# Two transformer blocks on one core: later-key sums of the first attention as three-row products in the short format, and the attention bias negated by ScalarE

## The reference

```python
for o in range(n):                      # key blocks of 128, nearest first
    z = einsum('bhnqd,bhnkd->bhnqk', qb[:, :, o:], kb[:, :, :n - o])
    log_rest = log_sigmoid(-z)
    if o == 0: log_rest = where(diag_mask, log_rest, 0.0)
    after = einsum('bhnqj,js->bhnqs', log_rest, after_mat) + carry[:, :, o:, :, None]
    w = exp(log_sigmoid(z) + after)
    ...
    carry = carry.at[:, :, o:].add(sum(log_rest, axis=-1))

scores = where(valid, scores + bias, -inf)     # chunked attention
```

## Time and profile before

| | |
|---|---|
| median of 3 runs | 697.48 us (697.42 to 697.54) |
| profiled execution, its own time | 697.37 us |
| its span | 695.6 us |
| mean granted TensorE clock | 0.998 |
| TensorE busy (PE) | 687.7 us, 99% |
| VectorE, ScalarE, GpSimd busy | 481.5, 406.3, 94.3 us |
| chain that ended last | PE 94%, POOL 2%, ACT 2%, DVE 1% |

### The profile page before, as it was taken

One profiled execution on the slowest core, in us unless ns is written; L12 is line 12 of the kernel. 1 busy time (PEld: TensorE's weight loads), 2 busy tenths in 40 slices (PEclk: granted clock), 3 DMA queues, 4 the chain that ended last, 5 costly groups with the idle time before them and its releaser, 6 DMA issues.

```text
span 695.6 us, 9577 instructions
## 1 busy us (share of the span) xinstructions
PE 687.7 (99%) x3890; PEld 594.3 (85%) x3890; DVE 481.5 (69%) x717; ACT 406.3 (58%) x680; POOL 94.3 (14%) x150
## 2 busy tenths in 40 slices
PE   9999999999999999999999999999999999999996
PEld 8888888888888888888888888998888888888885
DVE  6887687767666666667365767766668877777774
ACT  7776664657445555546555857554467665556553
POOL 2143022588200000002320000000000000000001
PEclk9999999999999999999999999999999999999999
DMA  9935533746555555536434334555454555445401
GB/s 342 387 122 207 217 119 125 256 175 216 203 186 184 188 197 203 196 122 221 175 126 175 122 122 182 189 183 201 155 188 175 191 214 200 182 182 183 180 1 60
DMA packets 19483, 126.13 MB, mean 181 GB/s; under 512 B 2416, under 2 KB 2544, under 8 KB 5232
## 3 DMA queue, kind: packets, MB, share of 16 engines
q1 hardware_dynamic: 19296, 125.34, 49.2%
q10 hardware_dynamic: 144, 0.20, 0.1%
HBM read 124.48 MB, written 1.05 MB: 180 GB/s over the span
## 4 chain that ended last, share of the span: by engine, by line
PE 94%; POOL 2%; ACT 2%; DVE 1%; issue 0%; POOLq 0%
PE bank L222 91%; PE bank L231 3%; POOL rtmp L243 1%; POOL qtok L243 0%; POOL ktok L243 0%; ACT whi L234 0%; DVE sc L1251 0%; DVE yy L251 0%; DVE xres L243 0%; DVE yy L243 0%; ACT L234 0%; ACT xa L234 0%; DVE wlo L243 0%; ACT sc L234 0%; ACT uT L234 0%
## 5 line engine op out<-in xcount | busy, mean ns | idle before, releaser
L243 DVE TENSOR_TENSOR wlo<-raw,whi 128x1024 fp32r<-128x1024 f32 x222 | 271.8, 1236 | 62.1 <-ACT whi L234 59.4
L234 ACT ACTIVATE whi<-raw 128x1024 fp32r<-128x1024 f32 x222 | 230.2, 1051 | 2.5 <-PE bank L222 2.1
L222 PE MATMUL bank<-xb,whi 128*128 128x512 f32 x496 | 124.3, 393 | 0.3 <-DVE sg L243 0.2
L222 PE MATMUL bank<-xa,whi 128*128 128x512 f32 (+1 forms) x496 | 115.7, 365 | 0.0
L222 PEld LDWEIGHTS bank<-xb,whi 128*128 128x128 f32 x496 | 90.4, 188 | 18.1 <-DVE sg L243 0.4
L222 PEld LDWEIGHTS bank<-xa,whi 128*128 128x128 f32 x496 | 87.4, 189 | 13.7
L222 PE MATMUL bank<-whi,xb 128*128 128x512 f32 (+1 forms) x352 | 96.5, 355 | 0.0
L222 PEld LDWEIGHTS bank<-xb,wlo 128*128 128x128 f32 x496 | 67.7, 190 | 4.9
L222 PEld LDWEIGHTS bank<-whi,xb 128*128 128x128 f32 x352 | 62.1, 189 | 9.3 <-ACT vtok L234 0.3
L222 PE MATMUL bank<-xa,wlo 128*128 128x256 f32 x432 | 69.4, 282 | 0.0
L222 PE MATMUL bank<-xb,wlo 128*128 128x256 f32 x496 | 69.1, 282 | 0.0
(11 more groups left out here) (235 smaller groups left out, 898.5 us busy)
## 6 DMA issues: line engine op xcount, KB each, us to landing
raw<-in_w_dram SPq DMA_DIRECT2D x109, 1024.0 KB, 4.8
first<-in_first_dram SPq DMA_DIRECT2D x8, 388.0 KB, 6.1
raw<-in_w_dram SPq DMA_DIRECT2D x4, 512.0 KB, 8.1
bias<-in_bias_dram SPq DMA_DIRECT2D x1, 1024.0 KB, 8.5
xres<-in_x_dram SPq DMA_DIRECT2D x1, 1024.0 KB, 6.8
gain<-in_ffn_norm_w_dram SPq DMA_DIRECT2D x1, 512.0 KB, 8.3
gain<-in_mix_norm_g_dram SPq DMA_DIRECT2D x1, 512.0 KB, 9.1
gain<-in_ffn_norm_g_dram SPq DMA_DIRECT2D x1, 512.0 KB, 5.3
```

What stands on the lines that cost most here:

```text
L222: return P(lambda e: e.matmul(o, l, r, start=start, stop=stop), *w, inc=inc)
L234: return A(lambda e: e.activation(o, i, f, **kw), *w)
L243: return q(lambda e: e.tensor_tensor(out=o, in0=a, in1=b, op=op), *w)
```

## The change

For the sums over later keys, `tri` and `negs` are rounded once, at the start, to the short format (`tri_r`, `negs_r`, two GpSimd casts of 128x128). A new function `sb_parts(b)`, handed to `later` behind `sb_scores(b)`, makes a high part of each `L` on ScalarE (`L_h`) and a low part on VectorE (`L_l`), 128x384 each. `sb_after` then does four short products per head: `tri_r` and `negs_r` by the high part, `tri_r` and `negs_r` by the low part, the `tri_r` ones on 384 columns at once. `L_h` lies over zm and `L_l` over sp, and the first `tri` and `negs` lie where `wk0` is.

The bias is no longer negated by GpSimd before group 2, but by one ScalarE copy with scale -1 behind the last unit of group 3; the memset of its corner is queued there too.

```diff
-    tri = N("tri", [128, 128])
-    negs = N("negs", [128, 128])
+    tri_r = N("tri_r", [128, 128], F32R)
+    negs_r = N("negs_r", [128, 128], F32R)
...
+    wk_at = (N.lo + 511) // 512 * 512
+    tri, negs = [at(wk_at + 512 * i, n, [128, 128]) for i, n in enumerate(("tri", "negs"))]
     wk = [N(f"wk{i}", [128, 384]) for i in range(8)]
+    L_h, L_l = [[at(wk_at + (4 * i + j) * 1536, f"L{j}{i}", [128, 384], F32R) for i in range(2)] for j in range(2)]
...
+    def sb_parts(b):
+
+        for i in range(2):
+            h, L = 2 * b + i, wk[4 * i + 2]
+            sb["Lh", h] = copy(L_h[i][:, :], L[:, :], sb["L", h], sb["g", h])
+        for i in range(2):
+            h, L = 2 * b + i, wk[4 * i + 2]
+            sb["Ll", h] = low(L_l[i][:, :], L[:, :], L_h[i][:, :], sb["Lh", h])
...
-            mm(o[:, 0:256], tri[:, :], L[:, 0:256], True, False, sb["L", h], tri_tok, neg_tok, *bank_free[bank])
-            mm(o[:, 128:256], negs[:, :], L[:, 256:384], False, True)
-            p = mm(o[:, 256:384], tri[:, :], L[:, 256:384], True, True, inc=True)
+        for i in range(2):
+            h, gm, bank = 2 * b + i, wk[4 * i + 3], 4 + i
+            o, hi, lo = pb[bank], L_h[i], L_l[i]
+            mm(o[:, 0:384], tri_r[:, :], hi[:, :], True, False, sb["Lh", h], tri_tok, neg_tok, *bank_free[bank])
+            mm(o[:, 128:256], negs_r[:, :], hi[:, 256:384], False, False)
+            mm(o[:, 0:384], tri_r[:, :], lo[:, :], False, False, sb["Ll", h])
+            p = mm(o[:, 128:256], negs_r[:, :], lo[:, 256:384], False, True, inc=True)
...
-    g = ts(G, flat(bias[:, :, :]), flat(bias[:, :, :]), -1.0, None, ALU.mult, None, bias_ld)
-    bias_tok = memset(bias[0:64, :, 192:256], BIG, g)
     for n, _ in enumerate(group_1(2, qb)):
...
             sb_scores(0)
+            later(lambda: sb_parts(0))
...
             sb_scores(1)
+            later(lambda: sb_parts(1))
         elif n == 2:
             qn = q_scaled()
+        else:
+            a = copy(flat(bias[:, :, :]), flat(bias[:, :, :]), bias_ld, scale=-1.0)
+            bias_tok = memset(bias[0:64, :, 192:256], BIG, a)
```

More of the change, by code:

```diff
@@ L556, in two_block_program @@
     g = memset(tri[:, :], -1.0)
-    tri_tok = select(tri[:, :], [[-1, 128]], ALU.is_gt, 0.0, 0, 1, g)
-    neg_tok = memset(negs[:, :], -1.0)
+    g = select(tri[:, :], [[-1, 128]], ALU.is_gt, 0.0, 0, 1, g)
+    tri_tok = G(lambda e: e.tensor_copy(tri_r[:, :], tri[:, :]), g)
+    g = memset(negs[:, :], -1.0)
+    neg_tok = G(lambda e: e.tensor_copy(negs_r[:, :], negs[:, :]), g)
     g = memset(sbmask[:, :, :], 0.0)
@@ L647, in sb_scores @@
             zm, sp, L, gm = wk[4 * i:4 * i + 4]
-            sb["L", 2 * b + i] = stt(L[:, :], zm[:, :], 0.0, sp[:, :], ALU.max, ALU.add, sb["sp", 2 * b + i])
+            v = stt(L[:, :], zm[:, :], 0.0, sp[:, :], ALU.max, ALU.add, sb["sp", 2 * b + i])
             sb["g", 2 * b + i] = stt(gm[:, :], zm[:, :], 0.0, sp[:, :], ALU.min, ALU.subtract)
-    def sb_after(b):
[L653 to L656, removed]
-            mm(o[:, 0:256], tri[:, :], L[:, 0:256], True, False, sb["L", h], tri_tok, neg_tok, *bank_free[bank])
-            mm(o[:, 128:256], negs[:, :], L[:, 256:384], False, True)
-            p = mm(o[:, 256:384], tri[:, :], L[:, 256:384], True, True, inc=True)
+            sb["L", 2 * b + i] = v
+    def sb_parts(b):
[5 more added lines that the diff above has]
+            sb["Ll", h] = low(L_l[i][:, :], L[:, :], L_h[i][:, :], sb["Lh", h])
+    def sb_after(b):
+        for i in range(2):
[5 more added lines that the diff above has]
+            p = mm(o[:, 128:256], negs_r[:, :], lo[:, 256:384], False, True, inc=True)
             v = tt(V, gm[:, :], o[:, 0:384], gm[:, :], ALU.add, p, sb["g", h])
```

## The result

The changed kernel takes 699.42 us (median of 8 executions, 699.02 to 699.77) against 697.45 for the kernel before on the same chip (8 executions, 697.04 to 697.77): a ratio of 1.0028, 95% interval 1.0019 to 1.0038. It is 2.0 us slower. 697.9 was forecast, and the range ended at 698.7.

A forecast was written before the change was run, and what follows sets the result against it. TensorE's queue was taken as the bound up to 60 us. It saves 1.22 us but waits 1.65 at `sb_out(2)`, which starts 0.4 later: 697.37 + 0.4 = 697.8, or 697.9 against the median; range 696.2 to 698.7.

The forecast's parts named there:

- What bounds the kernel: Up to 60 us TensorE's queue is the clock; shorter products save their full length unless TensorE has to wait.
- Part 1, the products: TensorE's later-key blocks shrink from 1.75 to 1.14 us, saving 0.53 in the first and 0.61 in the second.
- the 1.22 of the sum: TensorE's whole saving: 1.14 us from both blocks plus 0.08 of waiting at the first `sb_out`.
- Part 2, the first pair: New ScalarE copies and VectorE subtractions before the first `sb_out` cost nothing; the cover holds by 0.7 us.
- Part 3, the second pair: The bias copy in ScalarE's queue delays the Exps; TensorE waits 1.65 us at `sb_out(2)`, starting 0.4 us later than before.
- Behind this nothing new comes: After the second `sb_out`, the bias, corner memset, late splits, casts and DMA order add no further delay.
- So the 0.4 stays to the end: The 0.4 us later start of `sb_out(2)` carries unchanged to the kernel's end.
- The cover: Rival: ScalarE's 2.29 us idle before the last Exps absorbs the new work, keeping all 1.22: 696.25 us, chance 0.15.
- The short products do work at 128 columns: Rival claimed the opposite: no gain at 128 columns, 0.22 us each, a block 1.58, 698.35 us; chance 0.10.
- VectorE did not wait for GpSimd's power: Rival claimed it would: first-pair subtraction held by the power, TensorE waiting 2.3 us, 700.2 us; chance 0.06.
- The slow side: Over 0.2% slower, above 698.88 us: the GpSimd power rival and half of the unknown, chance 0.08.

The follow-up runs named there:

- e8: The change with its bias copy behind the third unit of group 4 and the second head norm queued behind the second `sb_after`: 696.12 us, ratio 0.9978.
- e1: The change with the bias negated by GpSimd as in the kernel before: 699.86 us, ratio 1.0032.
- e5: The kernel before with the bias on ScalarE and 1280 of its columns copied once more as plain delay: 699.37 us.
- e6: The changed kernel itself, unaltered, measured again: 699.28 us median of 9 executions.

## Why the prediction was wrong, step by step

- **What bounds the kernel: right.** TensorE's queue is the clock, and only its waits count.
- **Part 1, the products: right.** 1.14 was worked out for a block and 1.37 with the weight product behind it; 1.37 was measured. The pair of 384 and 128 columns repeats every 0.285 (0.175 + 0.11). How it divides between the two isn't shown: a 384 starts 0.06 after a 128, and a 128 some 0.22 after a 384, but the records overlap (0.39 long, some 0.23 apart). TensorE reached the second scores at 45.03 - 0.56 = 44.47, forecast 44.68. In e8, where TensorE waits at neither `sb_out`, `sb_out(2)` starts 1.44 us earlier than before (57.69 less an offset of 0.16, against 58.97), so all that the products save is a little more than the 1.22 of the sum.
- **Part 2, the first pair: right.** No wait there; e1 shows the other side, 1.5 us when GpSimd keeps the bias.
- **Part 3, the second pair: right within 0.25 us at each step.** Less the 0.56: mask addition 45.42 (forecast 45.63), `kb` 51.82 (52.05), bias 1.91 long (1.88), `whi_65` 55.81 (56.04), first Exp 58.61 (58.83), `sb_out(2)` 59.19 (59.4), a pause of 1.51 (1.65). The start moved by 0.22 where the sum had 0.4.
- **"Behind this nothing new comes" and "So the 0.4 stays to the end": this failed.** It took a pause of TensorE to cost its own length and no more. The term that was left out is the half clock behind it, 1.7 us in 15 of 17 executions. I had read the granted clock of 0.998 as given, though the change made TensorE idle where it had been busy since 1.1 us. The two executions without the fall took 697.43 and 698.24, on both sides of the forecast of 697.9; that the sum would have come out is shown by these two alone.
- **The rivals.** The cover did not hold, for the reason given against it. The short products do work at 128 columns. VectorE did not wait for GpSimd's power. The case that the rival named did not come up, since the subtraction started first, at 40.75 against 41.01; but the one at 44.44 started inside the power and took 1.23 as well. The slow side was right in sign and had another mechanism, and its chance of 0.08 was far too small. The range's upper end had no case in it for what a pause sets off.

What stays open: why a pause of 1.5 us is followed by half clock in some executions and not in others, and whether its share is really higher with the short products. The fixed 54.6 us suggest that it matters where the pause lies counted from the start of full pace, which scattered from 4.2 to 7.2 us between the traces. That is not shown, and it can't be all: the pause of e5's trace lay 52.8 to 54.2 us behind that start, that of e6's 51.9 to 53.4, and only e6's was followed by a fall. Where in the execution the pause lies was not varied on its own.

## What to carry to other kernels

Where TensorE is never idle, a new wait can have two prices: its own length, and what the granted clock does behind it; read the clock stretch by stretch before calling a small stall cheap, and look at the single executions for a second group. When a shorter product makes the busiest engine arrive earlier, every queue that feeds it must be walked again with the new arrival, and work that is moved to another engine belongs behind the instruction that the busy engine waits for next, not into idle time that lies on the far side of it. Here the same instructions in three orders gave 699.4, 696.8 and 696.1 us.

## What the runs showed of the hardware that was not expected

- TensorE's granted clock fell from 2.4 to 1.2 GHz for 3.4 us behind a pause of 1.5 or 2.2 us, with 1.2 to 2.1 us of work between the pause and the fall, in the three traces that have one. By the times of the executions it did so in 33 of 50 executions with pauses of 1.49 to 2.2 us and in none of 44 with pauses of 0.17 to 1.07. The fall costs 1.7 us in the trace, as much as the pause itself.
- In those three traces the fall lies 54.6 us behind the start of full pace, which itself comes at 5.7 to 7.2 us. Until then the products run at half pace, while the views print a granted clock of 1.00. This start moves the whole execution by half a microsecond.
- A ScalarE copy of 128x2048 took 1.91 us, GpSimd's multiplication of the same tile 5.41 with VectorE held beside it.
